# First block's attentions: scores as three split products, grouped-query heads first, latent turns inside the first steps, reciprocals turned in one transpose

## The reference, cut to what matters

```python
def attend(q, k, v, scale):
    s = jnp.einsum("bqkgd,blkd->bkgql", q, k).astype(jnp.float32) * scale
    p = jax.nn.softmax(s, axis=-1).astype(v.dtype)
    return jnp.einsum("bkgql,blkd->bqkgd", p, v)

# in layer(), first block
o_mla = blocked_attend(q_mla, concat(k_mla_c, k_mla_l), concat(v_mla_c, v_mla_l), MLA_QK ** -0.5)
o_gqa = blocked_attend(q_gqa, concat(k_gqa_c, k_gqa_l), concat(v_gqa_c, v_gqa_l), GQA_DIM ** -0.5)
x = x + gt1 * merge_branches(o_mla, o_gqa, o_four, gates, lp)
if update_ctx:                      # layer 0 only
    oc_mla = attend(qc_mla, k_mla_c, v_mla_c, MLA_QK ** -0.5)
    oc_gqa = attend(qc_gqa, k_gqa_c, v_gqa_c, GQA_DIM ** -0.5)
# merge_branches: g_mla*(o_mla @ w_br_mla) + g_gqa*(o_gqa @ w_br_gqa) + g_four*(o_four @ w_four), then @ w_o
```

## Time and profile before

| what | value |
|---|---|
| runs | 2531.73, 2533.69, 2535.77 us; median 2533.69 |
| profiled execution | span 2534.4 us from first to last instruction; no other time is listed for it |
| PE busy | 2434.9 us, 96% |
| DVE, ACT, POOL busy | 1635.4, 1318.0, 405.1 us |
| granted TensorE clock | mean 0.993 |

### The profile page before, as it was taken

How to read it: one execution, slowest core, us unless ns; L and a number is a source line. 1 busy time by engine, 2 the same in 40 slices (tenths; PEclk the granted TensorE clock), 3 DMA queues, 4 the chain that set the end, 5 groups by cost and what they waited for, 6 DMA issues and landing times. The chain is left out here.

```text
span 2534.4 us, 45823 instructions
## 1 busy us (share of the span) xinstructions
PE 2434.9 (96%) x17406; PEld 2158.2 (85%) x17406; DVE 1635.4 (65%) x2537; ACT 1318.0 (52%) x2157; POOL 405.1 (16%) x354
## 2 busy tenths in 40 slices
PE   6999999999899999999999999998999999999997
PEld 5876899898599988875899899887998799769986
DVE  3664787567577857774788466546665666576655
ACT  3444566454546645545466455445554554465544
POOL 1210211221031121111301211020110211011102
PEclk9999999999999999999999999999999999999999
DMA  8576466566245655474556566563466466535663
GB/s 277 187 228 213 152 192 193 167 190 205 78 134 175 200 168 162 151 241 164 161 182 192 175 219 201 163 207 109 136 198 199 150 199 203 162 101 161 195 202 116
DMA packets 332956, 450.43 MB, mean 178 GB/s; under 512 B 28192, under 2 KB 207392, under 8 KB 332768
## 3 DMA queue, kind: packets, MB, share of 16 engines
q1 hardware_dynamic: 332400, 446.32, 55.9%
q0 software_dynamic: 368, 1.57, 0.2%
HBM read 446.73 MB, written 1.05 MB: 177 GB/s over the span
## 5 line engine op out<-in xcount | busy, mean ns | idle before, releaser
L771 DVE TENSOR_TENSOR wlo<-raw,whi 128x1024 fp32r<-128x1024 f32 (+2 forms) x706 | 845.2, 1215 | 589.4 <-ACT whi L765 585.4
L765 ACT CAST whi<-raw 128x1024 fp32r<-128x1024 f32 (+2 forms) x776 | 768.1, 1007 | 637.2 <-PE S L1065 233.7
L1086 PE MATMUL S<-hhi,whi 128*128 128x256 f32 x1943 | 538.4, 277 | 1.4 <-ACT b_kT L1394 0.9
L1086 PE MATMUL S<-hlo,whi 128*128 128x256 f32 x1943 | 536.5, 277 | 1.2 <-DVE hlo L2054 1.1
L1086 PE MATMUL S<-hhi,wlo 128*128 128x256 f32 x1943 | 536.5, 277 | 0.0
L1086 PEld LDWEIGHTS S<-hhi,whi 128*128 128x128 f32 x1943 | 365.2, 188 | 2.4 <-ACT b_kT L1394 1.1
L1086 PEld LDWEIGHTS S<-hlo,whi 128*128 128x128 f32 x1943 | 365.1, 188 | 1.8 <-DVE hlo L2054 1.7
L1086 PEld LDWEIGHTS S<-hhi,wlo 128*128 128x128 f32 x1943 | 365.1, 188 | 0.0
L1086 PE MATMUL G<-hhi,whi 128*128 128x256 f32 x1084 | 301.1, 278 | 0.4 <-ACT hhi L1456 0.4
L1086 PE MATMUL G<-hlo,whi 128*128 128x256 f32 x1084 | 298.1, 278 | 0.1
L1086 PE MATMUL G<-hhi,wlo 128*128 128x256 f32 x1084 | 297.9, 277 | 0.0
(11 more groups left out here) (404 smaller groups left out, 4336.0 us busy)
## 6 DMA issues: line engine op xcount, KB each, us to landing
raw<-in_ffn_wi SPq DMA_DIRECT2D x352, 256.0 KB, 3.5
raw<-in_w_up SPq DMA_DIRECT2D x264, 256.0 KB, 3.8
modw<-in_w_mod SPq DMA_DIRECT2D x192, 256.0 KB, 4.6
raw<-in_w_in SPq DMA_DIRECT2D x192, 256.0 KB, 3.0
raw<-in_ffn_wo SPq DMA_DIRECT2D x160, 256.0 KB, 3.5
raw<-in_w_down SPq DMA_DIRECT2D x120, 256.0 KB, 3.5
raw<-in_a_wqkv SPq DMA_DIRECT2D x72, 256.0 KB, 3.1
raw<-in_w_o SPq DMA_DIRECT2D x48, 256.0 KB, 3.2
```

Of the source, the lines that this page charges most:

```text
L765: act.copy(whi[:, n0 % SPLIT, z, w], raw[:, n0 % RAW, z, w]).then_inc(hi_done, 1)
L771: eng.tensor_tensor(wlo[:, n0 % SPLIT, z, w], raw[:, n0 % RAW, z, w], whi[:, n0 % SPLIT, z, w].bitcast(F32), ALU.subtract)\
L1086: mm = pe.matmul(o, w, x, start=first and c == 0 and m == 0 and z == 0, stop=last and c == kc - 1 and z == len(terms) - 1, skip_group_chec ...
```

## The change

1. Scores of `own` attentions are three products of halves instead of one fp32 product. Queries and keys need a hi and a lo. For GQA, ACT casts all keys (`kghi`) and queries (`qghi`) and DVE subtracts (`b_kglo`, `b_qglo`) during the gate products. For MLA, ACT casts one pair of heads in each of the steps 5, 7, 9, 11 (`pair_hi`), between its exponentials and its copy of the turned bank, and POOL subtracts. The PE waits on `qk_lo`.
2. The GQA pairs are steps 0 to 7, the MLA pairs 8 to 15; branch weights and gates follow that order.
3. The transposes of `mlat` stand inside steps 0, 1 and 2 (2, 3 and 3 groups). As their source lies where the probabilities go, the first three steps put their probabilities into the raw weight buffer.
4. So SP loads the `w_mod` units first and the branch weights after the turns of the first three steps.
5. DVE writes the reciprocals spread to [128 x 128] (a ring of four), and PE turns that by one transpose instead of the two fp32 products. This holds for all five attentions, those of the second block too (8 and 16 steps).

```diff
+WOVEN = (0, 2, 5, 8)
+EARLY = len(WOVEN) - 1
+SPLIT_AT, SPLITS = 5, 2 + MLA_H
+RDEN = 4
...
     if st.name == "own":
-        return [("mla", c, c) for c in range(MLA_H // 2)] + [("gqa", c, MLA_H // 2 + c) for c in range(GQA_H // 2)]
+        return [("gqa", c, c) for c in range(GQA_H // 2)] + [("mla", c, GQA_H // 2 + c) for c in range(MLA_H // 2)]
...
@@ SP @@
                 if st.kind == "attn" and st.mod:
                     ahead = STAGES[STAGES.index(st) + 1]
-                    for k in range(ahead.units):
-                        load_unit(ahead, k, k, 0)
                     sp.wait_ge(bank_done[1], st.n)
                     for i in range(st.mod[2]):
                         load_mod(st, i)
+                    for s in range(EARLY):
+                        for q in turn_banks(st, s):
+                            sp.wait_ge(tr_done[q % 2], q // 2 + 1)
+                    for k in range(ahead.units):
+                        load_unit(ahead, k, k, 0)
...
@@ PE @@
+                def own_scores(s):
...
+                    for j, z in order_:
+                        q_hi_, q_lo_, k_hi_, k_lo_ = heads[j]
+                        q, k = ((q_hi_, k_hi_), (q_hi_, k_lo_), (q_lo_, k_hi_))[z]
+                        s0 = (2 * (s % 2) + j) * SN
+                        mm = pe.matmul(S[:, s0:s0 + nb * P], q, k, start=z == 0, stop=z == 2, skip_group_check=True)
+                    mm.then_inc(s_done, 1)
...
-                    for j in range(2):
-                        pe.matmul(G[j * DH:(j + 1) * DH, T + t * P:T + (t + 1) * P],
-                                  rden[:, m + j:m + j + 1].to_broadcast([P, DH]), ident, start=True, stop=True, skip_group_check=True)
+                    pe.matmul(G[:, T + t * P:T + (t + 1) * P], rden[:, (st.a + s) % RDEN, :], ident,
+                              start=True, stop=True, is_transpose=True, skip_group_check=True)
...
+                    if mlat and s < EARLY:
+                        if s == 0:
+                            pe.wait_ge(rows_ready, mlat.rr)
+                        turn_latent(mlat, *WOVEN[s:s + 2])
...
@@ ACT @@
+                        keys, k_hi, _ = shared_halves(own)
+                        act.copy(k_hi, keys).then_inc(qk_hi, 1)
+                        act.copy(qghi[:, :, :], qgT[:, :, :]).then_inc(qk_hi, 1)
...
+                        if mlat and s >= SPLIT_AT and (s - SPLIT_AT) % 2 == 0 and s - SPLIT_AT < MLA_H:
+                            pair_hi((s - SPLIT_AT) // 2)
                         if TURN_LAG <= s < n + TURN_LAG:
...
@@ DVE @@
                     over_units(dve, st, lambda k, j, i: split_weights(st, j, i, k, lo_and_rows))
+                    if st.part:
+                        own = own_of(st)
+                        keys, k_hi, k_lo = shared_halves(own)
+                        for z, (x, hi, to) in enumerate(((keys, k_hi, k_lo), (qgT[:, :, :], qghi[:, :, :], qglo[:, :, :]))):
+                            dve.wait_ge(qk_hi, splits_before(own) + z + 1)
+                            dve.tensor_tensor(to, x, hi.bitcast(F32), ALU.subtract).then_inc(qk_lo, 1)
                     for _ in rows_work:
                         pass
...
-                            dve.reciprocal(rden[:, m], den[:, m]).then_inc(rden_ready, 1)
+                            if s >= 2 + RDEN:
+                                dve.wait_ge(pair_done, (g - RDEN) // 2 + 1)
+                            dve.reciprocal(rden[:, g % RDEN, :].rearrange("p (e d) -> p e d", e=2), per_head(den[:, m], DH))\
+                               .then_inc(rden_ready, 1)
...
@@ POOL @@
+                        if st.name == "own" and p < MLA_H // 2:
+                            for z, (x, hi, to) in enumerate(pair_halves(st, p)):
+                                pool.wait_ge(qk_hi, splits_before(st) + 2 + 2 * p + z + 1)
+                                minus(to, x, hi).then_inc(qk_lo, 1)
```

More of the change, by code:

```diff
@@ L639, in follows_mod, with woven, own_of, splits_before @@
             return st.kind == "gates" and st.part == 1
+        def woven(st):
+            return st.kind == "mlat" and st.full
+        def own_of(st):
+            return next(z for z in STAGES[STAGES.index(st):] if z.kind == "attn")
+        def splits_before(st):
+            return SPLITS * owns.index(st)
+        def key_halves(to, st):
+            if st.s == LAT:
+                return to[:, :].rearrange("p (e n) -> p e n", e=2), None
+            both = to[:, :].rearrange("p (z e n) -> p z e n", z=2, e=2)
+            return both[:, 0], both[:, 1]
+        def shared_halves(st):
+            hi, lo = key_halves(kghi, st)
+            return kgT[:, :, 0:st.blocks * P], hi, kglo[:, :, :] if lo is None else lo
+        def pair_halves(st, m):
+            hi, lo = key_halves(kst[m % 2], st)
+            own = slice(2 * m, 2 * m + 2)
+            keys = kT1[0:QK, own, 0:st.blocks * P], hi[0:QK], klo[0:QK, own, :] if lo is None else lo[0:QK]
+            return keys, (qT1[0:QK, own, :], qst[m % 2][0:QK], qlo[0:QK, own, :])
+        def prob_of(st, s):
+            return raw[:, s, :, :] if st.mod and s < EARLY else prob[:, s % 3]
         def value_bank(st, p):
```

108 lines of the change are left out of this document (80 added, 28 removed).

## The result

The changed kernel takes 2570.16 us (median of 4 runs, 2568.43 to 2571.47), the kernel before 2533.99 beside it: ratio 1.0139, 95% interval 1.0126 to 1.0151. It is slower by 36 us. I had said slower by 12, at 2545.7 with a range up to 2556: the sign is right, the size a third of the real one.

What follows compares the result with a forecast made beforehand. PE sets the pace only in places; LAT0's GQA steps are bound by a loop through ACT. CTX -1, LAT0 2.4 + 0.5, LAT1 3 + 0.5, second block 5.6 + 1 make +12.0: 2545.7 us, range 2524 to 2556.

Steps and rivals of the forecast that it cites:

- CTX: CTX attention: early start lost to waiting for mod units, later savings offset by casts and reciprocals; -1 us, ends -3 and +3.
- second block: Second block's attentions: longer DVE reciprocals cost 5.6 us in the 16-head one and 1 in the 8-head one.
- Start of LAT0 and LAT1: First steps of both: DVE's two more subtractions delay rows and first score, PE stands 3.5 us; step 3 comes 1.7 later.
- the eight groups are hidden: Steps 0 to 2 of LAT0 and LAT1: transposes covered by waiting; start gains nothing, 1.7 us later.
- The half clock: Start of both LATs: PE's idle may bring half clock, 0 to 2 us each; 0.5 each added.
- Behind step 8: LAT0: two cast pairs cost 2.9 us, tail returns 0.5. LAT1: pairs with mod unit about 10 against 8.6, +3.
- POOL's subtractions cost nothing: MLA pairs: POOL's subtractions, 2.2 and 1.1 us a pair, end two steps ahead of their scores at no cost.
- The reciprocal: 128 columns on DVE take 1.1 us; DVE becomes the 16-head attention's bound, 0.8 for each of seven pairs.
- The scores: Split products at 0.227 us each: MLA step 1.36 instead of 1.82, grouped-query step 0.75 with two heads overlapping.
- savings come through: Whole kernel: PE's saved work of 25 us shows as time; 2509 whole, 2521 with LAT0 chained; chance 0.20.
- plain pass: DVE's reciprocal is one plain pass of 0.29 us, so the second block gains 1: 2538 us; chance 0.21.
- added waits: New waits at the LATs' start, half clock in three attentions and the iterative reciprocal add up: 2553 us; chance 0.15.

Runs made afterwards that it cites:

- e12: Changed kernel with plain fp32 scores again, without the casts and subtractions for them; head order, turns in the first steps and reciprocals as changed: 2556.22 us, 1.0089.
- e13: e12 with the MLA rows turned ahead of the attention again, as in the kernel before; head order kept: 2537.99 us, 1.0013.
- e10: Changed kernel with four plain, unused products for PE during its wait at the start of LAT0 and LAT1: 2567.96 us, 1.0129.
- e5: Changed kernel with PE's mod unit issued ahead of the turn of the same step instead of behind it: 2561.46 us, 1.0106.
- e1: Kernel before with the reciprocal part alone: 128 columns on DVE, set up by one PE transpose: 2536.89 us, 1.0011.
- e2: Changed kernel with the old reciprocals put back: 2 columns on DVE, two products on PE: 2562.44 us, 1.0115.
- e14: e13 with a 2-column reciprocal and a copy instead of the 128-column one, and the mod unit ahead of the turn in LAT0 and LAT1: 2533.44 us, 0.9994.
- e17: e15's edits with grouped-query heads first in LAT0 alone, MLA first in CTX and LAT1, against the kernel before: 2529.58 us, 0.9979.
- e15: Kernel before with a 2-column reciprocal, copy and one transpose, and the mod unit ahead of the turn in LAT0 and LAT1: 2532.16 us, 0.9994.
- e6: Changed kernel with the third product (low half of the query) left out of every first-block score: 2565.90 us, 1.0125.
- e4: Changed kernel with the two 1024-column subtractions of the grouped-query halves moved from DVE to POOL: 2589.09 us, 1.0219.

## Why the prediction was wrong, by its steps

Sum: CTX forecast -1, came +5.1; LAT0 +2.9, came +9.9; LAT1 +3.5, came +9.5; second block +6.6, came +4.3. The remaining 3 us of span lie elsewhere: 2.0 ahead of CTX's attention, 1.6 between LAT0 and LAT1, and 0.5 less behind LAT1.

- **Start of LAT0 and LAT1: the step that failed first.** I put step 3 1.7 us later; it was 4.9 and 4.7. PE's idle was nearly as said (4.24 against 3.5), the wait for ACT in step 1 too. What failed is my sentence that the eight groups are hidden, by waiting: I let mod unit 0 start at 624.5, in the time of the kernel before; on the same scale it started at 625.8, at half clock. The larger error was to look for the cause in DVE's two subtractions. e12 has none, and the start is as long, since the mod weights then bind (3.90 us of wait). e13 shows the cause itself: 7 to 8 us of first third for the turning inside the steps. That is more than the 4.9 and 4.7 because the cheap grouped-query steps win some back (e13 has 16.2 and 17.0 for 18.2 in the kernel before). Before, the transposes hid the transfer; woven in, PE waits for the transfer first and does most of the transposes behind it.
- **The half clock** was in the sum with 0.5 a LAT and as 1.9 in a rival. It came in both (mod units of 2.83 and 3.32 us). But e10, which gave PE work through the gap and had the full clock, gained nothing that could be told, since the transfer came next; a full price for the clock would have named the wrong cause.
- **Behind step 8: the larger miss against the sum.** Forecast for LAT0 was 2.9 for casts, less 0.5; it came 6.9. For LAT1 I walked the pair at about 10 for two pairs; it was 10.6 for three. I had the loop (exponentials, casts, copy, turn) and put it beside PE's work; in a pair with a mod unit, unit, turn and values stand in the loop as well. e5 shows the unit's part: 4.1 behind step 8 of LAT1, 2.8 ahead of it. e12 sizes the splitting there, casts less what PE saves: 1.4 in LAT1, 4.5 in LAT0, where the lead weights and the turns that POOL and DVE take stand beside it. What stays in e12, 5.4 in LAT1, is mostly MLA steps of 3.92 us (two starts below) where grouped-query ones of 3.35 stood, eight of them: 4.6. This is the head order, which I had weighed in one sentence and not in the sum. It mostly moves time: e13 against e1, which differ by the order of heads and of loads, has 3.9 less ahead of step 8 of LAT1 and 4.9 more behind it.

```profile
1174.72 1.99 PE L1249 MATMUL S<-b_kT,b_qT 96*128 96x512 f32 x4
...
1178.64 1.98 PE L1249 MATMUL S<-b_kT,b_qT 96*128 96x512 f32 x4
```

- **"POOL's subtractions cost nothing."** They end in time, as said, but DVE's 1.22 us subtraction took 3.20 beside them, and its followers waited.
- **CTX**: the first mod unit arrived late and ran at half clock, as said (row below); the second, said to be late too, waited for no transfer and took 1.92 us (185.59). The early start was given to waiting, 4.66 us, and three steps in CTX was 0.9 behind, by the same woven turns (e13 has 18.9 there for 20.7). The last third lost 4.3. e12 and e2 have 38.4 for 40.4, which points at casts and long reciprocals; but e14 has neither and is at 40.0, while e17, MLA first there, is at 36.1 (e15: 37.8). So about half of it or more is the head order; what casts and reciprocals add can't be told from the spread.

```profile
178.06 3.64 PE L1029 MATMUL G<-modw,silz 128*32 128x512 f32 x16 [4.66 <-DMA modw<-in_w_mod]
```

- **The reciprocal**: the mechanism was right and the price nearly so (0.94 measured for 1.1). The 8 ns an element of a 2-column row was a good guide: (942 - 155) / 126 is 6.2 ns. The 16-head attention lost 3.4, not 5.6: two steps take 4.73 with DVE busy 4.66, where I had 5.3.
- **The scores**: 0.227 a product was right, and that two heads on different rows overlap: a grouped-query step of after takes 0.89 us from its first product to the turn (0.75 said), an MLA step about 1.5 (1.36 said). That little of this reaches the time was right too, and e6 sizes it: about a third or less.

```profile
654.88 0.51 PE L1256 MATMUL S<-kghi,qghi 64*128 64x512 f32 x2
655.21 0.40 PE L1256 MATMUL S<-b_kglo,qghi 64*128 64x512 f32 x2
655.44 0.40 PE L1256 MATMUL S<-kghi,b_qglo 64*128 64x512 f32 x2
655.77 1.09 PE L1203 MATMUL TB<-consts,raw 128*128 128x128 f32 x8
```

- The rival "savings come through" is dead by PE's idle time; "plain pass" by the 942 ns; "added waits" had two of the right waits and reached 2553, 17 short.

What stays open: why the mod unit ahead of the turn brings the half clock to CTX (e5), and where the 2 us ahead of CTX's attention come from. They seem to go with the split scores: the last gates product ends at 168.1 to 171.1 us in every kernel that has them, and at 166.4 to 168.2 in the others.

## What to carry to other kernels

Work that seems to stand in the way at a stage's start may be what covers a transfer. Before it is moved, ask what PE does in the time in which the next weights arrive. When a loop runs through several engines and two steps, write it once around, with everything that PE's queue puts between its own two links; an independent piece of PE's work belongs ahead of the instruction that waits, not behind it. It pays only where the wait is real: LAT1 won 6.5 us by it in e5, while e15 as a whole can't be told from the kernel before. Put the cheap steps where nothing else is hidden, and the dear ones where the engine waits anyhow.

## What I had not expected of the hardware

- A reciprocal of 128 fp32 columns takes 942 ns on DVE and a copy of as many 235; two columns take 155.
- DVE and POOL took turns on subtractions from SBUF: 0.29 us became 2.38 (e4), 1.22 became 3.20, and POOL's 1.3 became 2.25.
- Two split (fp32r) products of 64 rows and 512 columns on different rows of the array start every 0.23 us as a pair (655.21 to 655.44), as often as single ones of 96 rows (1189.46 to 1189.69).
